# Small-block groups one chunk earlier, and the last remainder of each pass's down weights made by GpSimd

## What is computed

```python
def expert_block(args):
    idx, gate, e = args
    xb = xt[idx]
    g = jnp.minimum(xb @ w_gate[e] + b_gate[e], SWIGLU_LIMIT)
    u = jnp.clip(xb @ w_up[e] + b_up[e], -SWIGLU_LIMIT, SWIGLU_LIMIT)
    act = g * jax.nn.sigmoid(SWIGLU_ALPHA * g) * (u + 1)
    y = act @ w_down[e] + b_down[e]
    return y * gate[:, None].astype(y.dtype)
```

## Time and profile before

| | |
|---|---|
| runs, median (lowest to highest) | 2213.45 us (2213.32 to 2217.33), 3 runs |
| profiled execution, its own time | 2214.42 us |
| its span, first to last instruction | 2212.7 us |
| busy: PE, DVE, ACT, POOL | 97%, 70%, 50%, 40% |
| mean granted TensorE clock | 0.988 of full speed |
| iterations 1 to 29 of the loop | 873.07 to 2152.45 us |
| an iteration without small work, with three groups | 37.3 to 40.6 us, 49.4 us |

### The profile page before, as it was taken

One profiled execution on the slowest core, in us unless ns is written; L12 is line 12 of the kernel. 1 busy time (PEld: TensorE's weight loads), 2 busy tenths in 40 slices (PEclk: granted clock), 3 DMA queues, 4 the chain that ended last, 5 costly groups with the idle time before them and its releaser, 6 DMA issues.

```text
span 2212.7 us, 37038 instructions
## 1 busy us (share of the span) xinstructions
PE 2137.0 (97%) x11540; PEld 1557.8 (70%) x11541; DVE 1538.9 (70%) x1940; ACT 1114.8 (50%) x1138; POOL 888.5 (40%) x486
## 2 busy tenths in 40 slices
PE   8999999999999969999999999999999999999997
PEld 6874554787888847777666767776776766677776
DVE  5544433535335588988777788878887877789996
ACT  4433233424222146675645656565665655566674
POOL 1343121000000045875633545555574455356761
PEclk9999999999999979999999999999999999999999
DMA  6421110233334289999878898899898898899994
GB/s 227 98 74 60 39 47 10 82 90 102 88 105 152 105 325 388 352 357 338 302 274 292 315 303 317 307 319 313 308 352 280 302 307 291 291 318 324 351 341 111
DMA packets 206010, 517.77 MB, mean 234 GB/s; under 512 B 19168, under 2 KB 86624, under 8 KB 205952
## 3 DMA queue, kind: packets, MB, share of 16 engines
q1 hardware_dynamic: 190016, 470.97, 59.2%
q0 software_dynamic: 15936, 46.02, 8.6%
HBM read 480.68 MB, written 32.05 MB: 232 GB/s over the span
## 4 chain that ended last, share of the span: by engine, by line
PE 69%; issue 8%; DVE 8%; POOL 8%; DMA 3%; DVEq 3%; ACT 1%; SPq 0%; POOLq 0%; ACTq 0%
PE psum L1689 7%; PE psum L1933 7%; PE psum L1924 6%; PE psum L1926 6%; PE psum L1901 5%; POOL pick L679 4%; PE psum L1709 4%; PE psum L1711 4%; PE psum L1710 4%; DVE late_lo L1385 3%; PE psum L1964 3%; PE psum L1966 3%; PE psum L1972 3%; PE psum L1912 2%; DMA out_rows<-ysb,idx_cur 2%
## 5 line engine op out<-in xcount | busy, mean ns | idle before, releaser
L679 POOL TENSOR_SCALAR pick<-iota_bf,slot_col 128x256 bf16<-128x256 bf16 x244 | 523.5, 2160 | 214.5 <-DVE slot_col L1403 214.5
L1385 DVE TENSOR_TENSOR late_lo<-late_raw,w_hi 128x2048 fp32r<-128x2048 f32 x192 | 433.2, 2291 | 121.9 <-PE psum L1972 83.2
L1385 DVE TENSOR_TENSOR ring_lo<-ring,w_hi 128x2048 fp32r<-128x2048 f32 x191 | 432.6, 2300 | 70.2 <-PE psum L1933 70.2
L922 ACT ACTIVATE w_hi<-late_raw 128x2048 fp32r<-128x2048 f32 x192 | 363.4, 1918 | 1.3 <-DMA late_raw<-in_w_up 0.8
L922 ACT ACTIVATE w_hi<-ring 128x2048 fp32r<-128x2048 f32 x192 | 354.2, 1922 | 9.9 <-DMA ring<-in_w_up 9.9
L1924 PE MATMUL psum<-w_hi,xT_hi 128*128 128x512 f32 x992 | 270.4, 394 | 0.8 <-DVE idx_new L1379 0.5
L1926 PE MATMUL psum<-w_hi,xT_lo 128*128 128x512 f32 x992 | 265.6, 389 | 0.0
L1924 PEld LDWEIGHTS psum<-w_hi,xT_hi 128*128 128x128 f32 x992 | 184.1, 188 | 46.5 <-issue 7.4
L1926 PEld LDWEIGHTS psum<-w_hi,xT_lo 128*128 128x128 f32 x992 | 186.2, 188 | 39.5
L1689 PE MATMUL psum<-hT,ring 128*128 128x512 f32 x384 | 174.2, 601 | 0.0
L653 POOL TENSOR_TENSOR rstd<-var,half 128x1 f32<-128x1 f32 x8 | 4.4, 554 | 409.5 <-DVE var L1327 409.5
(11 more groups left out here) (362 smaller groups left out, 3706.0 us busy)
## 6 DMA issues: line engine op xcount, KB each, us to landing
late_raw<-in_w_down SPq DMA_DIRECT2D x132, 512.0 KB, 4.6
ring<-in_w_gate SPq DMA_DIRECT2D x130, 512.0 KB, 4.3
ring<-in_w_up SPq DMA_DIRECT2D x130, 512.0 KB, 5.4
late_raw<-in_w_gate SPq DMA_DIRECT2D x126, 512.0 KB, 6.0
late_raw<-in_w_up SPq DMA_DIRECT2D x126, 512.0 KB, 7.7
ring<-in_w_down SPq DMA_DIRECT2D x124, 512.0 KB, 5.0
ring<-in_w_in SPq DMA_DIRECT2D x44, 512.0 KB, 5.1
ring<-in_x SPq DMA_DIRECT2D x16, 512.0 KB, 4.0
```

The costliest lines, as they stand in the source:

```text
L679: e.tensor_scalar(pick[:, t, :], iota_bf[:, :], slot_col[:, t, :], None, ALU.is_equal).then_inc(g_pick, 1)
L922: e.activation(w_hi[:, hs, :], raw_of(c0), ACT.Copy).then_inc(g_hi, 1)
L1385: e.tensor_tensor(lo_of(c0), raw_of(c0), w_hi[:, hs, :].bitcast(F32), ALU.subtract).then_inc(g_lo, 1)
```

## The change

Six edits in the loop, and what follows from them at its end:
- The second gate and up group of a small block moves from chunk 10 (k = 2) to chunk 9 (k = 1), its down group from chunk 14 (k = 6) to 13 (k = 5), the first group of the next block from chunk 19 to chunk 18. The signals move with them. `rows_transpose` moves from behind chunk 17 to behind chunk 16.
- The remainder of chunk 19 is made on POOL, behind the picks, the wait for ACT's rounding, a read of the flag and, with a small block, the wait for its down group. A semaphore of its own, `g_lo_pool`, tells PE; DVE's `g_lo` counts 11 a pass.
- `slots_of` moves on DVE from behind chunk 12 to the head of the iteration.
- `row_numbers` moves on DVE from ahead of chunk 20's remainder to behind it.
- In `gate_up` bank 3 is written last, and the wait for the row numbers stands ahead of it.

```diff
@@ gpsimd, the loop
                 pick_tokens(p + 3)
+                hold(e, g_hi, 12 * p + 20)
+                hb = e.value_load(table[0:1, bass.ds(p + NT, 1)], min_val=0, max_val=1)
+                with e.If(hb > 0):
+                    hold(e, g_small, 3 * p + 5)
+                e.tensor_tensor(lo_of(19), raw_of(19), w_hi[:, 19 % SPLIT, :].bitcast(F32), ALU.subtract).then_inc(g_lo_pool, 1)
                 with e.If(p > 0):
                     scattered(p)
@@ vector, the loop
+                slots_of(p + 3, exn)
                 for k in range(1, 4):
                     rest_of_weights(p, 8 + k)
                 swiglu(p, hb)
                 small_taken(hbn, 3 * p + 4)
                 rest_of_weights(p, 8 + 4)
-                slots_of(p + 3, exn)
...
                 evacuate(p + 1, hbn, 12 * p + 16)
-                for c in range(2, 4):
-                    rest_of_weights(p, 16 + c)
+                rest_of_weights(p, 16 + 2)
                 rest_of_rows(p + 2, xT_hi, xT_lo, 0)
                 shift_rows(p, False)
-                row_numbers(p + 3, 3)
                 small_taken(hb2, 3 * p + 6)
                 rest_of_weights(p, 12 + 8)
+                row_numbers(p + 3, 3)
@@ tensor, gate_up
-                for i in range(4):
+                for i in range(3):
                     if halves and i == 2:
                         e.wait_ge(g_ev, 2 * p + 2)
-                    if numbers is not None and i == 3:
-                        e.wait_ge(g_rows, numbers)
                     e.matmul(bank[i][:, :], hi[:, k, :], w_hi[:, hs, 512 * i:512 * i + 512], start=(k == 0), stop=False)
-                for i in range(4):
+                for i in range(3):
                     e.matmul(bank[i][:, :], lo[:, k, :], w_hi[:, hs, 512 * i:512 * i + 512], start=False, stop=False)
+                if numbers is not None:
+                    e.wait_ge(g_rows, numbers)
+                e.matmul(bank[3][:, :], hi[:, k, :], w_hi[:, hs, 1536:2048], start=(k == 0), stop=False)
+                e.matmul(bank[3][:, :], lo[:, k, :], w_hi[:, hs, 1536:2048], start=False, stop=False)
                 if aside:
                     aside()
...
-                e.wait_ge(g_lo, at + 1)
+                e.wait_ge(g_lo, 11 * p + (c0 + 1))
@@ tensor, down
-                e.wait_ge(g_lo, at + 1)
+                if of_pool is not None:
+                    e.wait_ge(g_lo_pool, of_pool)
+                else:
+                    e.wait_ge(g_lo, 11 * p + (c0 + 1))
@@ tensor, the loop
-                    gate_up(p, 8 + k, k, aside={2: second_rows, 6: down_rows}.get(k), signals_small=k in (2, 6))
+                    gate_up(p, 8 + k, k, aside={1: second_rows, 5: down_rows}.get(k), signals_small=k in (1, 5))
...
-                    down(p, 16 + c, c, aside={1: third_expert, 3: next_rows}.get(c), signals_small=c == 3)
-                    if c == 1:
+                    down(p, 16 + c, c, aside={1: third_expert, 2: next_rows}.get(c), signals_small=c == 2, of_pool=p + 1 if c == 3 else None)
+                    if c == 0:
                         rows_transpose(p + 2, 0, 2)
```

More of the change, by code:

```diff
@@ L343, in build @@
         first_lo = sem("first_lo")
-        g_warm = sem("g_warm"); g_hi = sem("g_hi"); g_lo = sem("g_lo"); g_chunk = sem("g_chunk"); g_small = sem("g_small")
+        g_warm = sem("g_warm"); g_hi = sem("g_hi"); g_lo = sem("g_lo"); g_chunk = sem("g_chunk"); g_small = sem("g_small"); g_lo_pool = sem("g_lo_pool")
         g_bgu = sem("g_bgu"); g_bd = sem("g_bd")
@@ L1957, in act_transpose, with down @@
                 ins.then_inc(g_atr, 1)
-            def down(p, c0, c, aside=None, signals_small=False):
+            def down(p, c0, c, aside=None, signals_small=False, of_pool=None):
                 at, slot, hs, _ = chunk_at(p, c0)
@@ L2068, in part @@
                     if h == 0:
-                        e.wait_ge(g_lo, at + 1)
+                        e.wait_ge(g_lo, 11 * n_loop + (21 + c))
                     for k in (2 * c, 2 * c + 1):
@@ L2101, in _ @@
             for k in range(1, GU_CHUNKS):
-                gate_up(n_loop, 8 + k, k, aside={2: last_second_rows, 6: last_down_rows}.get(k), signals_small=k in (2, 6))
+                gate_up(n_loop, 8 + k, k, aside={1: last_second_rows, 5: last_down_rows}.get(k), signals_small=k in (1, 5))
                 if k == 3:
```

## The result

| | median, us | runs | ratio to before |
|---|---|---|---|
| before | 2213.94 | 4 | |
| after | 2246.28 | 4 | 1.0147 (1.0134 to 1.0159) |

A forecast was written before the change was run, and what follows sets the result against it. PE, busy 97% of the span, was taken as the bound, so only its waits could give time back. Terms -15.7 + 6.0 + 3.2 (waits for ut) + 0.7 = -5.8 us, from the median 2213.45, gave 2207.6; range 2198 to 2219.

The forecast's parts named there:

- 1.10 for the loop's four table loads: On DVE ahead of slots_of and chunk 9: the loop's four register loads were counted at 1.10 us, from the earlier trace.
- D: How far into PE's pass DVE's chunk 9 begins; forecast 2.35 us without a next small group, PE losing about D - 0.5.
- 0.28 to 1.1: Bounds in us for one register load, between POOL's wait for ACT's rounding and its subtraction; 0.7 was taken.
- The small groups, -15.7: Start of 15 passes: an earlier next small group releases DVE's chunk 8 sooner, ending PE's waits, 1.05 us a pass.
- The new wait at rows_transpose, +6.0: Behind chunk 16, PE waits for DVE's evacuation of ut, 0.4 us in 15 passes that also evacuate a small block.
- without the small block the evacuation ends 0.6 sooner and nothing waits: At rows_transpose in passes evacuating no small block: DVE's evacuation of ut ends 0.6 us sooner, so no new wait.
- No wait of PE goes directly: Small down group from chunk 14 to 13: DVE's chunks 16 and 17 start 2.7 us sooner, no direct gain for PE.
- The subtraction: Chunk 19's remainder on POOL: 4.6 us, ending 10.5 after down's first chunk starts, 2 us before PE needs it.
- Passes without small work, +0.7: DVE-bound passes: cycle 39.3 us against 38.94, costing 1.8 over five, less 1.1 for picks' waits that go.
- Bank 3 last, nothing: Order inside gate_up: same matmuls and weight loads, row numbers ready in time, one more register instruction a chunk; no cost.
- GpSimd comes later: Rival, chance of slower 0.18: subtraction ends later in 15 passes, 13 us per us; at 1.1 us later, 2222.

## Why the prediction was wrong

- *The failed step.* "1.10 for the loop's four table loads" as the whole cost of the loads, used again after the row numbers had been moved between chunk 8 and the loads. The 1.10 was a gap, what was left of 3.3 us behind 2.29 of cover; the edit took the cover. Term: 3.19 measured for 1.10, +2.1 in D in all passes without a next small group. The edit alone is worth 32 us in the changed kernel and 82 in the kernel before. The prediction did not ask what hid a part of this idle time and what it would be bare. The clue was there: "1.10 <-ACT w_hi" in the earlier trace rows and "1.13 <-issue" in the earlier trace rows both stand directly behind chunk 8's remainder of 2.29, and the trace of the kernel before holds the loads themselves, 0.72 apart. The same reading gave the bounds "0.28 to 1.1" for one load; that 0.7 was near the 0.64 measured on POOL was luck.
- *The small groups, -15.7.* Right: 15.7 once the transposes' wait is out of the way.
- *The new wait at rows_transpose, +6.0.* Right, 5.3, in the passes it was worked out for. Missed: about nine more in the passes without small work, where the transposes wait 1.4 each for DVE's evacuation. The sentence "without the small block the evacuation ends 0.6 sooner and nothing waits" took DVE to be waiting for PE.
- *The small down group, "No wait of PE goes directly".* Wrong, in the good direction: 3.4 us in five passes, by DVE's earlier chunk 9 behind it.
- *The subtraction.* 4.62 against 4.6; its end 0.4 late, by a gap of 1.06 for 0.7; chunk 8 0.65 behind it for 0.25. That it is covered by PE's later need was right: no wait of PE for chunk 19 shows. That DVE's path through it costs little was wrong in size: 5.8 us in the mildest surroundings tried (row numbers first, POOL's load ahead of the picks), 11.7 with rows_transpose later, 29.6 in the changed kernel itself (2246.28 against 2216.71), where it overlaps with the first step.
- *Passes without small work, +0.7.* Wrong: a cycle of 41.97 instead of 39.3. 2.1 are the loads; the subtraction, started behind ACT, which is itself behind DVE's evacuation, and the 1.4 at rows_transpose are in the rest, whose shares were not separated.
- *Bank 3 last, nothing.* The kernel with the groups put back and bank 3 last has passes of 46.38 and 49.8 where the kernel before with `slots_of` at the head has 46.38 and 49.8. Right for the matmuls. Left out of the account: PE's three loads now stand behind the wait for the row numbers and are bare for 1.65 us in 15 passes; DVE's late chunk 9 hid this.
- *The rival "GpSimd comes later".* It had the right place, DVE's chunk 9 in the passes without a next small group, and nearly the right slope (13 us per us; chunk 9 came 2.7 us late and the time 38.7 above the forecast, 14 per us), with the wrong cause. A term read in one surrounding only, times this slope, should have widened the range upwards.

## What to carry to other kernels

An idle time ahead of an instruction is not the price of what stands there but what the operation before it did not cover: before moving anything between a register load and the long operation ahead of it, add that operation's length back. Put such loads behind a long operation that nothing later in the queue has to wait for (here two or four of them, worth some 15 us in 30 passes, together with 0.5 us of work moved with them), and never behind a wait that is met late. An operation handed to GpSimd that shares DVE's path can cost more than it frees: it was a loss in all four pairs here, 5.8 to 29.6 us. That it would gain where DVE has nothing to do meanwhile on the chain that counts was not tried.

## What the runs showed of the hardware

- A register load costs 0.7 us on DVE (3.19 for four, 1.82 for two; 0.72 between their records, beside an operation or alone), 0.75 between records on PE and 0.64 on POOL; loads in a row add up, and an instruction behind them waits whether it uses them or not.
- DVE's queue passes loads while its engine works; the nine short operations of the row numbers, with waits on DVE's own semaphores among them, left it no lead, and 3.19 us stood bare behind them against 1.02 behind a remainder.
- A copy of 128x2 beside POOL's 128x2048 subtraction took 3.25 us, against 0.16 in the kernel before, while two operations that read PSUM, started beside it, kept their 1.29 for two; the picks took 2.8 us each on average in the changed kernel (677.8 for 244). In the kernel before, the 95 picks with no remainder of DVE beside them took 0.91 to 0.93 each, the 152 with one 2.57 at the middle and up to 4.92; the remainders stayed at 2.3.
